# Retention heads with V as the stationary operand, their norm through VectorE's block transposes and a fold matmul, and two PSUM banks for the attention units' V products

## The reference

```python
CHUNK = 64; RET_HEADS = 4; RET_HEAD_DIM = 128
att = jnp.einsum("bnihd,bnjhd->bnhij", qc, kc) * intra_decay[None, None]
o_intra = jnp.einsum("bnhij,bnjhe->bnihe", att, vc)
...                                  # o_inter: the state carried over from earlier chunks
o = rms_norm_2(o_intra + o_inter)    # over a head's 128 features, eps 1e-6
...
y = concat([ya * silu(ag), yr * silu(rg)], axis=-1)
return x + y @ w_out
```

## Time and profile before

| | |
|---|---|
| median of 3 runs | 1198.65 us (1197.14 to 1198.66) |
| the profiled execution | 1195.86 us |
| its span, first to last instruction | 1193.6 us |
| PE busy | 1179.8 us, 99%, 5813 matmul records |
| PEld busy | 999.4 us, 84% |
| DVE busy | 870.6 us, 73% |
| ACT busy | 592.5 us, 50% |
| POOL busy | 260.1 us, 22% |
| granted TensorE clock | 0.999 of full speed |

### The profile page before, as it was taken

The page is one execution under the profiler, slowest core; times in us unless marked ns, Lnnn a source line. Parts: engine busy times, 40 slices in busy tenths (PEclk is TensorE's granted clock), DMA queues, the critical chain, the costliest instruction groups (busy, mean ns, idle before and its releaser), DMA issues.

```text
span 1193.6 us, 15642 instructions
## 1 busy us (share of the span) xinstructions
PE 1179.8 (99%) x5813; PEld 999.4 (84%) x5813; DVE 870.6 (73%) x1417; ACT 592.5 (50%) x1067; POOL 260.1 (22%) x283
## 2 busy tenths in 40 slices
PE   9999999999999999999999999999999999999998
PEld 7887788888888888888888889899888889899886
DVE  6789855656786578546776788887867788988746
ACT  6777623234343344324435477755445577754542
POOL 0220499932000000000004511012323311012300
PEclk9999999999999999999999999999999999999999
DMA  6455433333422433243333366652213376663621
GB/s 191 143 169 170 142 101 94 88 106 89 139 77 68 140 106 89 72 124 104 90 102 92 104 189 183 194 161 72 84 58 109 98 209 199 173 175 116 158 71 71
DMA packets 218767, 146.84 MB, mean 123 GB/s; under 512 B 6250, under 2 KB 209476, under 8 KB 218564
## 3 DMA queue, kind: packets, MB, share of 16 engines
q1 hardware_dynamic: 218692, 145.86, 42.4%
HBM read 127.49 MB, written 18.35 MB: 122 GB/s over the span
## 4 chain that ended last, share of the span: by engine, by line
PE 86%; DVE 7%; ACT 5%; issue 2%; DMA 0%; DVEq 0%; POOL 0%; ACTq 0%; POOLq 0%
PE ps L191 85%; ACT a_p L161 1%; DVE tmp L164 1%; DVE a_p L178 1%; ACT whi L161 1%; ACT b_p L161 1%; ACT b_sets L161 1%; DVE wlo L164 1%; DVE a_pd L182 1%; DVE x1h L167 1%; PE ps L194 1%; DVE a_zc L167 0%; DVE tmp L167 0%; ACT x1h L161 0%; DVE b_pt L164 0%
## 5 line engine op out<-in xcount | busy, mean ns | idle before, releaser
L161 ACT ACTIVATE whi<-raw 128x1024 fp32r<-128x1024 f32 (+1 forms) x198 | 206.3, 1050 | 281.6 <-PE ps L191 270.3
L164 DVE TENSOR_TENSOR wlo<-raw,whi 128x1024 fp32r<-128x1024 f32 (+1 forms) x192 | 248.7, 1302 | 47.9 <-ACT whi L161 46.9
L191 PE MATMUL ps<-x0h,whi 128*128 128x512 f32 x1008 | 254.5, 391 | 1.8 <-ACT whi L161 1.8
L191 PE MATMUL ps<-x0h,wlo 128*128 128x512 f32 x1008 | 254.4, 391 | 0.0
L191 PE MATMUL ps<-x0l,whi 128*128 128x512 f32 x1008 | 254.2, 390 | 0.0
L191 PEld LDWEIGHTS ps<-x0l,whi 128*128 128x128 f32 x1008 | 188.2, 188 | 39.1 <-DVE x0l L167 0.5
L191 PEld LDWEIGHTS ps<-x0h,whi 128*128 128x128 f32 x1008 | 187.1, 188 | 39.8 <-ACT whi L161 2.0
L191 PEld LDWEIGHTS ps<-x0h,wlo 128*128 128x128 f32 x1008 | 187.7, 188 | 38.1
L164 POOL TENSOR_TENSOR sums<-sums,sq 128x512 f32<-128x512 f32 x28 | 43.3, 1559 | 416.7 <-ACT sq L161 416.7
L191 PE MATMUL ps<-x1h,wlo 128*128 128x512 f32 x304 | 82.3, 389 | 0.0
L191 PE MATMUL ps<-x1h,whi 128*128 128x512 f32 x304 | 82.3, 389 | 0.0
(11 more groups left out here) (188 smaller groups left out, 1659.1 us busy)
## 6 DMA issues: line engine op xcount, KB each, us to landing
raw<-in_w_in_dram SPq DMA_DIRECT2D x98, 512.0 KB, 4.3
raw<-in_w_up_dram SPq DMA_DIRECT2D x44, 512.0 KB, 3.8
raw<-in_w_out_dram SPq DMA_DIRECT2D x24, 512.0 KB, 3.9
turned<-b_pd SPq DMA_DIRECT2D x16, 640.0 KB, 3.2
raw<-in_w_down_dram SPq DMA_DIRECT2D x16, 512.0 KB, 4.0
b_px<-turned SPq DMA_DIRECT2D x32, 160.0 KB, 3.6
b_p<-turned SPq DMA_DIRECT2D x32, 160.0 KB, 3.5
turned_a<-a_pd SPq DMA_DIRECT2D x6, 512.0 KB, 2.6
```

Of the source, the lines that this page charges most:

```text
L161: return AC.put(lambda e: e.activation(o, i, func, **kw), after, AC, 1)
L164: return on.put(lambda e: e.tensor_tensor(o, a, b, op), after, on, 1)
L191: return PE.put(lambda e: e.matmul(o, l, r, start=start, stop=stop), after, PE if mark else None, 1)
```

## The change

A retention head keeps its scores, decays and halves. Its V product makes V the stationary operand: four pairs of matmuls with V hi and V lo stationary and P hi moving (512, 384, 256 and 128 columns), then four with V hi stationary and P lo moving, 12 matmuls into bank 7, one step later than before and with the lo half of P read last. The result has features on the partitions, so the four transposes go. The norm is made from a copy and a square (ACT), `blocks` and `add_up` (DVE), a matmul with `FOLD` into bank 6 (bank 5 for the last head), the reciprocal root over 128x16 (its first operation on DVE, since it reads PSUM; the other 11 or so on POOL, or on DVE for the last head), `spread` and a product on DVE. The fourth head's V product falls one step into the output projection.

Head 6 of the attention half starts at step 49 instead of 48. A third buffer joins those of the retention heads, so the copy of `RB2` (`keep_rb2`, `h_final`) moves from `PX` to `PD`. In the first block the units' V products alternate between banks 6 and 7. The two first transfers, `mix_norm` and the identity, are issued by ACT instead of SP.

```diff
-        t_mix = dma(rows[0][0:8, :], ..., d_mix)
-        t_id = dma(CA[:, 0:128], const_a[:, 0:128], d_id)
+        t_mix = dma(rows[0][0:8, :], ..., d_mix, on=AC)
+        t_id = dma(CA[:, 0:128], const_a[:, 0:128], d_id, on=AC)
...
-            o, free = PS[7], claim(7)
+            o, free = PS[6 + u], claim(6 + u)
...
-            bank_free[7] = [a1, a2]
+            bank_free[6 + u] = [a1, a2]
...
-        ... rps = ..., Slots(p_bufs, [0, 1], p_free)
+        ... rps = ..., Slots(p_bufs, [0, 1, 2, 0], p_free)
...
                 tl.append(tt(lo[:, 1024:1280], pb[:, 1024:1280], f32(hi[:, 1024:1280]), ALU.subtract, after=[th[2], tfree]))
-                yield 1
-                ends, free = [], [claim(3), claim(4)]
-                for t in range(4):
-                    o = PS[3 + t // 2][:, 256 * (t % 2):256 * (t % 2) + 256]
-                    for kt in range(t + 1):
-                        c = PT_K[kt] + 128 * (t - kt)
-                        mm(o, hi[:, c:c + 128], v_at(s // 2, kt)[:, s % 2, :], kt == 0, False, after=[th, tl, tok_v[s // 2], free[t // 2]])
-                        tp = mm(o[:, 0:128], lo[:, c:c + 128], v_at(s // 2, kt)[:, s % 2, 0:128], False, kt == t, mark=kt == t)
-                    ends.append(tp)
+                yield 2
+                o, free = PS[7], claim(7)
+                vs = [v_at(s // 2, kt)[:, s % 2, :] for kt in range(4)]
+                for kt in range(4):
+                    c, a0 = 128 * kt, PT_K[kt]
+                    mm(o[:, c:512], vs[kt][:, 0:128], hi[:, a0:a0 + 512 - c], kt == 0, False, after=[th, tok_v[s // 2], free])
+                    mm(o[:, c:512], vs[kt][:, 128:256], hi[:, a0:a0 + 512 - c], False, False)
+                for kt in range(4):
+                    c, a0 = 128 * kt, PT_K[kt]
+                    tp = mm(o[:, c:512], vs[kt][:, 0:128], lo[:, a0:a0 + 512 - c], False, kt == 3, after=tl, mark=kt == 3)
...
-                t1 = [act(tmp[h], both[h][:, :, 128:256], after=[ends[2 * h + 1], th, tl]) for h in range(2)]
-                yield 1
-                t2 = [tt(ob[h], both[h][:, :, 0:128], tmp[h], ALU.add, after=[t1[h], tl]) for h in range(2)]
-                yield 1
-                for t in range(4):
-                    t3 = act(tmp[t // 2][:, t % 2, :], ob[t // 2][:, t % 2, :], ACT.Square, accum=sc[:, t:t + 1], after=t2[t // 2])
-                rr, t4 = rsqrt_of(sc, 4, 1.0 / 128, 1e-6, t3, on=PO)
-                yield 3
-                t5 = [act(ob[t // 2][:, t % 2, :], ob[t // 2][:, t % 2, :], scale=rr[:, t:t + 1], after=t4) for t in range(4)]
-                yield 1
-                for t in range(4):
-                    tp = tr(PS[7][:, 128 * t:128 * t + 128], ob[t // 2][:, t % 2, :], IDENT, after=[t5[t], free], mark=t == 3)
-                yield 1
...
-                t3 = tt(t, PS[7][:, :], s2, ALU.mult, after=[tp, ts2, free])
+                t1 = act(out, o[:, :], after=[tp, th, tl])
+                t2 = act(sq, o[:, :], ACT.Square, after=[tp, th, tl])
+                bank_free[7] = [t1, t2]
+                yield 1
+                k, t, free = T.take()
+                t3 = blocks(t, sq, after=[t2, free])
+                t3 = add_up(part, t.rearrange("p (j b) -> p j b", b=32), after=[t3, tl])
+                yield 1
+                bank = 5 if i == 3 else 6
+                tp = mm(PS[bank][:, 0:16], FOLD[:, :], part, True, True, after=[t3, va["fold"], claim(bank)], mark=True)
+                yield 1
+                rr, t4, t_read = rsqrt_of(PS[bank][:, 0:16], 16, 1.0 / 128, 1e-6, tp, on=DV if i == 3 else PO, c=c, read=DV)
+                if i < 3:
+                    yield 3
+                t5 = spread(sq, rr, t4)
+                t6 = tt(out, out, sq, ALU.mult, after=[t5, t1])
+                yield 1
...
+                t3 = tt(t, out, s2, ALU.mult, after=[t6, ts2, free])
...
-                at_step(13 - l + 6 * i if i == 0 else 12 + 6 * i, head(i))
+                at_step(49 if i == 6 else 12 + 6 * i, head(i))
```

More of the change, by code:

```diff
@@ L194, in tr, with dma @@
             return PE.put(lambda e: e.transpose(o, i, ident), after, PE if mark else None, 1)
-        def dma(o, i, done, after=()):
-            return SP.put(lambda e: e.dma_start(o, i), after, done, 16)
+        def dma(o, i, done, after=(), on=None):
+            return (on or SP).put(lambda e: e.dma_start(o, i), after, done, 16)
         agenda, step_no, n_prod = {}, [0], [0]
@@ L349, in tiles, with rsqrt_of @@
             return a.rearrange("p (t c) -> p t c", c=128)
-        def rsqrt_of(src, n, scale, eps, after, on=DV, c=None):
+        def rsqrt_of(src, n, scale, eps, after, on=DV, c=None, read=None):
             c = cols(3 * n) if c is None else c
             v, y, a = c[:, 0:n], c[:, n:2 * n], c[:, 2 * n:3 * n]
-            t = ts(v, src, scale, eps, ALU.mult, ALU.add, after=after, on=on)
+            t = ts(v, src, scale, eps, ALU.mult, ALU.add, after=after, on=read or on)
+            t_read = t
             if n == 32:
@@ L370, in rsqrt_of @@
                     t = tt(y, a, y, ALU.mult, after=t, on=on)
-            return y, t
+            return (y, t) if read is None else (y, t, t_read)
         diag_free = []
@@ L481, in block_then_hybrid_layers @@
         t_ones = memset(ONES[:, :], 1.0)
-        t_mix = dma(rows[0][0:8, :], mix_norm[0].rearrange("(a b) -> a b", b=128), d_mix)
-        t_id = dma(CA[:, 0:128], const_a[:, 0:128], d_id)
+        t_mix = dma(rows[0][0:8, :], mix_norm[0].rearrange("(a b) -> a b", b=128), d_mix, on=AC)
+        t_id = dma(CA[:, 0:128], const_a[:, 0:128], d_id, on=AC)
         t_x = []
@@ L1362, in keep_rb2 @@
             def keep_rb2():
-                t = act(PX[:, 0:512], RB2[:, :], after=[rb["rb2"], p_free[2]])
+                t = act(PD[:, 0:512], RB2[:, :], after=[rb["rb2"], pd_free[0]])
                 slot_free[5].append(t)
@@ L1369, in h_final @@
             def h_final(k):
-                h_tok[k] = stt(Hk(k), Hk(k), FIN(k), PX[:, 0:512], ALU.mult, ALU.mult, after=[rb2c, h_read[k]])
-                p_free[2] = [h_tok[k]]
+                h_tok[k] = stt(Hk(k), Hk(k), FIN(k), PD[:, 0:512], ALU.mult, ALU.mult, after=[rb2c, h_read[k]])
+                pd_free[0] = [h_tok[k]]
                 yield
@@ L1434, in ret @@
                 yield 1
[L1436 to L1439, removed]
-                t1 = [act(tmp[h], both[h][:, :, 128:256], after=[ends[2 * h + 1], th, tl]) for h in range(2)]
+                out, sq, part, c = pb[:, 0:512], pb[:, 512:1024], pb[:, 1024:1040], pb[:, 1040:1088]
@@ L1444, in ret @@
+                T.free[k] = [t3]
                 yield 1
-                sc = cols(4)
-                for t in range(4):
-                    t3 = act(tmp[t // 2][:, t % 2, :], ob[t // 2][:, t % 2, :], ACT.Square, accum=sc[:, t:t + 1],
-                             after=t2[t // 2])
-                rr, t4 = rsqrt_of(sc, 4, 1.0 / 128, 1e-6, t3, on=PO)
-                yield 3
-                t5 = [act(ob[t // 2][:, t % 2, :], ob[t // 2][:, t % 2, :], scale=rr[:, t:t + 1], after=t4)
-                      for t in range(4)]
@@ L1458, in ret @@
+                bank_free[bank] = [t_read]
+                if i < 3:
+                    yield 3
+                t5 = spread(sq, rr, t4)
+                t6 = tt(out, out, sq, ALU.mult, after=[t5, t1])
                 yield 1
@@ L1462, in ret @@
                 k, t, free = T.take()
-                t3 = tt(t, PS[7][:, :], s2, ALU.mult, after=[tp, ts2, free])
-                bank_free[7] = [t3]
+                t3 = tt(t, out, s2, ALU.mult, after=[t6, ts2, free])
+                rps.free[kp] = [t3]
                 s2s.free[k3] = [t3]
```

5 lines of the change are left out of this document (1 added, 4 removed).

## The result

The kernel became slower. Its four runs have a median of 1205.12 us (1203.33 to 1205.89), against 1197.89 us (1196.16 to 1198.66) for the kernel before; the ratio is 1.0058, with a 95% interval of 1.0046 to 1.0070. The prediction was 1191.8 us, between 1189 and 1197, and had given "slower" a chance of 0.05. The profiled execution took 1205.89 us, with a span of 1203.8 and a mean clock of 0.993.

The account below looks back on a forecast made before the run. TensorE, busy 99% of the span, was taken as the bound. Retention 5.1, V product's wait 0.6, attention 1.0 and start 0.15 gave 6.85 us, so 1198.65 - 6.85 = 1191.8 us, range 1189.0 to 1197.0.

Parts of the forecast that it names:

- Its sum of TensorE's work: Retention heads: transposes 3.8 plus V product 3.2 less fold 1.9 give 5.1 us; 0.6 more from the V product's wait.
- The move of head 6: Attention half: starting head 6 a step later changes its matmuls' place, not their number; costed at nothing.
- The rival that only columns count: Retention V product: turning the operands saves nothing, since weight loads hide behind neighbouring matmuls; 1195.0 us, chance 0.03.
- I cost it at nothing, and the cover is this: Retention norm: 2.1 us more VectorE work a head costs TensorE nothing; three steps cover the fold, 17.2 us the last head.
- the waits that the prediction named as signs of its being wrong: Retention stretches: TensorE waiting for `b_sets`, `wlo` or the fold's operand would show the prediction wrong; no size given.
- The V product did take over 2.1 us: Retention V product: expected 1.86 us a head; over 2.1 us was a sign of the prediction being wrong.
- The slower rival: Retention stretch: VectorE becomes the bound, its `spread` waiting for GpSimd's root; 1.5 us a head, 1203.8 us, chance 0.05.
- The attention's 1.0 us: Attention units: two banks remove the fifth and sixth V products' wait for `tmp`; 1.0 us gained, ends 0.5 and 3.6.
- +0.15: Start: x is issued some 0.84 us earlier, of which at most about 0.15 us comes through as gain.
- a loss of 1.3: Start, lower end: ScalarE issues only after its 1.28 us table load; up to 1.3 us lost if the identity lands last.
- The difference was carried over: Whole kernel: the runs' median lies 2.8 us above the profiled execution of 1195.86 us; the same difference kept for the forecast.

Follow-up runs that it names:

- the best version: Start undone, first layer's output projection in banks 1, 2, 0, 6, second's beginning in bank 6, last pair of heads one group later in the first layer: 1189.43 us.
- the run with the root on VectorE: Changed kernel with the first two transfers back on SP and the third retention head's reciprocal root on VectorE instead of GpSimd: 1204.29 us.
- the start undone: Changed kernel with the mix row's and the identity's transfers issued from SP again: 1202.29 us.
- the banks alone: Kernel before the change, with only the attention units' V products in banks 6 and 7: 1196.22 us.
- the run with the start alone: Kernel before the change, with only the mix row's and the identity's transfers issued from ScalarE's queue: 1200.20 us.
- the run with the spread later: Changed kernel, first two transfers back on SP, third head's spread a step later, last pair of heads one group later in the first layer: 1198.57 us.

## Why the prediction was wrong, point by point

**Its sum of TensorE's work was about right.** Without the stop the two layers are 3.1 + 3.3 = 6.4 us shorter in the profile of the best version; the prediction had 5.1 + 0.6 = 5.7. The two are not made up alike, though. The move of head 6, costed at nothing, took away a wait for `b_sets` of 0.42 us in each layer of the kernel before, which the earlier trace rows leaves out:

```profile
PE ps L191 <- DVE b_sets L164: 0.8, 2, 0.4
```

From the sixth head's scores to the eighth's, with head 6 itself (the seventh) between them, the layers are shorter by 0.69 and 0.64 us (27.65 and 27.60 before, 26.96 in both after). So some 1.3 us of the 6.4 belong to this move, and about 5.1 are left for the retention heads, where 5.7 were reckoned. The rival that only columns count falls with the 1.86 us of the new V product.

**The step that failed is "I cost it at nothing, and the cover is this".** It followed what the norm itself hands back to TensorE, the fold and the halves of `X1`, and found 2.8 and 6 us of room; these held, with no wait before the fold of any consequence. It did not ask what else VectorE does for TensorE behind the norm's new instructions. That was the evacuation of bank 0, which had 0.89 us to spare, and its cover was the V product, which the change moved by a step, a move costed at nothing too. None of the waits that the prediction named as signs of its being wrong (`b_sets`, `wlo`, the fold's operand) came. The V product did take over 2.1 us, 2.57 in the first layer, but only because the clock was low behind the stop. The loss is 8.7 us of standing and about 4.2 us of half clock in the profile, against 6.4 saved: 6.5 more for the two layers, where the table has 4.4 + 2.2.

**The slower rival had part of the mechanism, but the wrong victim and too small a chance.** It said that the `spread` would wait on VectorE for GpSimd's root and hold up what is queued behind. This is what the rows at 880.87 show. It looked for the victim among `wlo`, the rotary products and the lo halves, and priced it by head; it was a bank, once in a layer. That its 1203.8 us lies close to the measured 1205.12 is chance: it came from eight waits of 1.5 us, and the trace has two of 5.1 and 3.6 with half clock behind them. Its argument against, some 8 us of free time on VectorE and three steps for the root, did not hold: GpSimd's chain took 874.48 to 880.84, 6.4 us, more than three steps of 1.82; the third head's root over 128x4 had already taken 865.89 to 871.54, 5.65 us, in the kernel before. And free time earlier in a stretch doesn't help an instruction that stands behind a late one. By the run with the root on VectorE the wait isn't the whole of it either.

**The attention's 1.0 us was right, the clock apart.** The profiles of the start undone and of the banks alone both show -1.0; the timed runs give 1.6 and 2.0 us for the two banks, and the interval of the first holds 1.0. In the changed kernel's own profile 1.6 us of half clock behind the second wait turned it into +0.5. That fall isn't tied to the two banks: in the 14 profiles the clock fell behind these units 7 times, in 5 of the 10 with two banks and in 2 of the 4 with one.

**The start was mis-signed.** +0.15 was taken, and a loss of 1.3 kept as the other end. That end was right by luck: it was the length of ScalarE's table load, behind which the issues were to stand, but ScalarE issued at 0.71 and 1.36 and loaded its table only at 1.76. What was late was the identity's landing, 5.0 us after its issue in the changed kernel. This costs 1.05 to 1.27 us in the two profiles with the move. In time the move costs 1.8 us by the run with the start alone, and 3.5 (0.29% of 1198) by the difference of the changed kernel and the start undone. Some of the rest is slow matmuls behind it: in both, the first pair of wide matmuls took 1.22 us. But the same happened in some profiles with the transfers on SP. How much of the start's 3.1 us in the one profile belongs to the change is therefore not settled beyond these two differences.

**The baseline was a lucky execution.** The sum was made against an execution 2.8 us below the median, and its start was one of the faster ones. The difference was carried over as the prediction said, so this did no harm.

## What to carry to other kernels

Saving work on the bounding engine brings it sooner to the next thing it must wait for, so look for the first hand-over behind the savings, here a PSUM bank, and ask which engine's queue gives it free and what stands ahead of that instruction. A matmul group that seems to be moved for nothing may be covering such a hand-over. Where one bank is freed last, begin with another and end in one that the next stage doesn't start with: four digits in two lists turned +0.29% (the start undone) into -0.41%, and bank 0 third with bank 6 last in the first layer, with the last heads read a group later, turned it into -0.73%.

## What the runs showed of the hardware

The pace of the first matmuls differs between executions whose start is the same code. With the first transfers on SP, the first two wide matmuls took 0.73 or 0.74 us in six profiles and 0.87 to 1.22 in six others. The granted clock from 10 to 15 us stood at 1.00 in five of these twelve and at 0.52 to 0.88 in seven, and the first `tmp<-ps,rb` of VectorE started anywhere from 33.24 to 36.33 us. So a single profile can't weigh an edit at the start. In the two profiles with the transfers on ScalarE the clock reads 1.00 from 5 to 15 us, although the pair took 1.22 us there; the record of the clock does not show every slow stretch of the start.

A wait of 1.0 us behind one of 0.8, in the attention units with two banks, was followed by half clock in five executions and by full clock in five others, with the same instructions. Behind the stop of 5.10 us the clock stood at 0.50 from 885 to 890 us and at 0.91 in the next 5 us; in the run with the spread later, whose stop of 3.38 us ended at 880.82, it stood at 0.66 from 880 to 885 us and at 1.00 in the next 5.
